# The entries of the feed-forward and MLP stages by token tile, and the gating units in single banks

## The reference

```python
x = x + rms_norm(h, norm_mix_post[i])
h = conv_gated_ffn(rms_norm(x, norm_ffn_pre[i]), ffn_w_in[i], ...)
# gating unit: 3072 features u and 3072 features v
z = jax.nn.gelu(h @ w_in)
u, v = jnp.split(z, 2, axis=-1)
v = layer_norm(v, ln_g, ln_b)            # over 3072 features
sv = einsum("gts,bcsgd->bctgd", tril(w_s), v) + b_s
return (u * sv) @ w_out
# MLP
f = jnp.square(jax.nn.relu(h @ w_up)) @ w_down
```

## Time and profile before

| | |
|---|---|
| median of 3 runs | 1098.77 us (1098.67 to 1100.65) |
| the profiled execution | 1098.5 us, its span 1096.7 us |
| instructions | 18812 |
| TensorE, VectorE, ScalarE busy | 97%, 74%, 61% |
| DMA | 185 MB, mean 169 GB/s |

### The profile page before, as it was taken

One profiled execution on the slowest core, in us unless ns is written; L12 is line 12 of the kernel. 1 busy time (PEld: TensorE's weight loads), 2 busy tenths in 40 slices (PEclk: granted clock), 3 DMA queues, 4 the chain that ended last, 5 costly groups with the idle time before them and its releaser, 6 DMA issues. The chain is left out here.

```text
span 1096.7 us, 18812 instructions
## 1 busy us (share of the span) xinstructions
PE 1069.3 (97%) x6166; PEld 912.2 (83%) x6166; DVE 814.1 (74%) x1427; ACT 669.0 (61%) x1246; POOL 39.8 (4%) x71
## 2 busy tenths in 40 slices
PE   7999999999999999999999999999999998999997
PEld 7977888888788998887888888899668887888886
DVE  6777988888744457886988888798779748666664
ACT  6666555555845855667555455777777756555543
POOL 0110000000010002220000000000000000000000
PEclk9999999999999999999999999999999999999999
DMA  8463665555466375442666656265212545655541
GB/s 330 136 218 121 206 215 186 184 192 183 133 246 192 126 231 163 154 153 78 228 201 200 191 175 195 84 221 173 77 39 79 186 141 171 190 184 187 189 153 38
DMA packets 51379, 185.03 MB, mean 169 GB/s; under 512 B 5728, under 2 KB 6240, under 8 KB 51328
## 3 DMA queue, kind: packets, MB, share of 16 engines
q1 hardware_dynamic: 49248, 178.28, 49.4%
q0 software_dynamic: 1504, 5.44, 1.5%
q10 hardware_dynamic: 576, 0.64, 0.2%
HBM read 183.29 MB, written 1.05 MB: 168 GB/s over the span
## 5 line engine op out<-in xcount | busy, mean ns | idle before, releaser
L156 DVE TENSOR_TENSOR w_lo<-raw,w_hi 128x1024 fp32r<-128x1024 f32 x336 | 415.3, 1245 | 85.3 <-ACT w_hi L151 82.0
L151 ACT ACTIVATE w_hi<-raw 128x1024 fp32r<-128x1024 f32 x336 | 350.0, 1053 | 81.1 <-PE ps L228 45.0
L198 PE MATMUL ps<-both,w_hi 128*128 128x512 f32 x960 | 341.9, 399 | 1.4 <-DVE both L436 1.4
L228 PE MATMUL ps<-w_hi,both 128*128 128x512 f32 x992 | 293.5, 396 | 6.0 <-DVE both L1264 2.4
L200 PE MATMUL ps<-both,w_lo 128*128 128x256 f32 x960 | 269.8, 281 | 0.0
L198 PEld LDWEIGHTS ps<-both,w_hi 128*128 128x128 f32 x960 | 180.5, 188 | 45.7 <-issue 2.0
L228 PEld LDWEIGHTS ps<-w_hi,both 128*128 128x128 f32 x992 | 178.8, 188 | 45.4 <-issue 3.4
L200 PEld LDWEIGHTS ps<-both,w_lo 128*128 128x128 f32 x960 | 181.6, 189 | 2.5
L228 PE MATMUL ps<-w_lo,both 128*128 128x512 f32 x496 | 158.3, 392 | 0.0
L173 PE MATMUL ps<-both,w_hi 128*128 128x256 f32 x448 | 128.8, 287 | 0.8 <-DVE arena L400 0.7
L174 PE MATMUL ps<-both,w_hi 128*128 128x256 f32 x448 | 126.9, 283 | 0.0
(11 more groups left out here) (202 smaller groups left out, 1119.0 us busy)
## 6 DMA issues: line engine op xcount, KB each, us to landing
raw<-in_w SPq DMA_DIRECT2D x336, 512.0 KB, 3.6
row<-in_rows POOLq DMA_DIRECT2D x7, 512.0 KB, 4.7
x<-in_x SPq DMA_DIRECT2D x2, 512.0 KB, 4.3
out<-x SPq DMA_DIRECT2D x4, 256.0 KB, 2.0
misc<-in_misc POOLq DMA_DIRECT2D x1, 512.0 KB, 6.1
arena<-in_ws POOLq DMA_DIRECT2D x1, 512.0 KB, 9.0
tab<-in_tables POOLq DMA_DIRECT2D x1, 320.0 KB, 4.7
tab<-in_tables POOLq DMA_DIRECT2D x1, 256.0 KB, 5.0
```

Source lines behind the costliest of these rows:

```text
L151: act.activation(w_hi[:, s, :], raw[:, s, :], ACT.Copy).then_inc(hi_done, 1)
L156: dve.tensor_tensor(w_lo[:, s, :], raw[:, s, :], w_hi[:, s, :].bitcast(F32), ALU.subtract).then_inc(lo_done, 1)
L198: pe.matmul(ps[:, bank, :].rearrange("p (h t) -> p h t", h=2), w_hi[:, s, c], both[:, :, k, :], start=k == 0, stop=False)
L228: mm = pe.matmul(ps[:, 2 * tt + c, :], a[:, slot, t], b[:, s, c * 512:(c + 1) * 512], start=f, stop=z)
```

## The change

- **Entries** (updates 0, 2, 4). `settle` and its dummy products go. `entry_pe` takes the sublayer's first two units apart by token tile with `features_tile`: tile 0 of unit n, half of the k of tile 0 of unit n + 1, then the transposes of tile 1, the other half, then tile 1 of both units. A k of a tile has a product of 256 columns (2 x 128) and one of 128, each with its own weight load. The feed-forward's row product comes one unit later, in bank 2; tile 0's gate and up banks are 0 and 1; tile 1 of x is transposed to banks 6, 7, 2, 3 at updates 0 and 2.
- **Weight halves.** At updates 0, 2 and 4 ScalarE makes the high halves of units n0 + 2 and n0 + 3 around the halves of x's tile 1 and VectorE their low halves behind them; units 4 and 5 come after the update. Update 4 takes the early order (both next squares behind those halves). The MLP's first three steps make two halves each in place of a block ahead of them.
- **Gating units.** u is made by `features_apart`, one unit to a bank (7, 0, 3 by turns). ScalarE copies the right half to `pad`, VectorE adds it to the left half into SBUF, multiplies a pair by ROW there, and ScalarE takes the gelu in place. A bank is free after the sum. The first output unit goes by token tile: tile 0 waits for the sum of unit 22, tile 1 for that of unit 23. The first three spatial products come two units later.
- **Squares by chunk.** A chunk's squares are taken one chunk later, about the chunk's own mean (`MID`); VectorE corrects them at the end to the common mean, by 512 times the square of the means' difference.

```diff
+    def features_tile(pe, n, bank, tt, pre, ks=range(KT)):
+
+        s = n % RING
+        pe.wait_ge(lo_done, n + 1)
+        o = ps[:, bank, :].rearrange("p (h t) -> p h t", h=2)
+        for k in ks:
+            pe.wait_ge(pre.lo, pre.base + k + 1)
+            c = slice(k * P, (k + 1) * P)
+            pe.matmul(o[:, :, tile(tt)], w_hi[:, s, c], both[:, :, k, tile(tt)], start=k == 0, stop=False)
+            mm = pe.matmul(o[:, 0, tile(tt)], w_lo[:, s, c], a_hi[:, k, tile(tt)], start=False, stop=k == KT - 1)
+        if tt == TT - 1:
+            mm.then_inc(unit_used, 1)
+
+    def entry_pe(pe, u, n, banks):
+
+        early, late = (Pre(u.next.lo, KT * (TT * u.n + tt)) for tt in range(TT))
+        features_tile(pe, n, banks[0], 0, early)
+        features_tile(pe, n + 1, banks[1], 0, early, range(KT // 2))
+        turn_tile_pe(pe, u, 1)
+        features_tile(pe, n + 1, banks[1], 0, early, range(KT // 2, KT))
+        features_tile(pe, n, banks[0], 1, late)
+        features_tile(pe, n + 1, banks[1], 1, late)
...
-    def spun(tt, k):
-
-        bank, c = (6, 7, 1, 2)[k // 2] if tt else 4 + k // 4, k % 2 if tt else k % 4
+    def spun(u, tt, k):
+
+        right = (6, 7, 2, 3) if u.n in (0, 2) else (6, 7, 1, 2)
+        bank, c = right[k // 2] if tt else 4 + k // 4, k % 2 if tt else k % 4
         return ps[:, bank, c * P:(c + 1) * P]
...
-    def update_act(act, u, g, following, early):
+    def update_act(act, u, g, following, early, ahead=RING):
...
+            if ahead == HELD:
+                hi_to(act, u.n_last + 3)
             hi_tile_act(act, u, 1, g)
+            if ahead == HELD:
+                hi_to(act, u.n_last + 4)
         next_act(act, u, 1)
         if following is not None:
             act.preload_act_table(following)
-        hi_to(act, u.n_last + RING)
-
-    def update_dve(dve, u, g, r, early, rows=None):
+        hi_to(act, u.n_last + ahead)
+
+    def update_dve(dve, u, g, r, early, rows=None, ahead=RING):
...
+        if early or ahead == HELD:
+            lo_to(dve, u.n_last + 4)
         if early:
-            lo_to(dve, u.n_last + 4)
             next_inverse(dve, u, 0)
         next_inverse(dve, u, 1)
         if rows is not None:
-            row_dve(dve, rows, 1)
-        lo_to(dve, u.n_last + RING)
+            lo_to(dve, u.n_last + 5)
+            row_dve(dve, rows, 2)
+        lo_to(dve, u.n_last + ahead)
...
-        return (0, 3) if t == 0 and isinstance(i, int) else (4 + t % 2, 6 + t % 2)
+        return (0, 1) if t == 0 and isinstance(i, int) else (4 + t % 2, 6 + t % 2)
     def ffn_pe(pe, f, n0, u, following, turn_early=True):
-        features_apart(pe, n0, 0, pre=after(u))
-        row_pe(pe, u, 1)
-        features_apart(pe, n0 + 1, 3)
-        ffn_in_pe(pe, f, n0, 1)
+        entry_pe(pe, u, n0, f_banks(0, 0))
+        features_apart(pe, f_g(n0, 1), f_banks(1, 0)[0])
+        row_pe(pe, u, 2)
+        features_apart(pe, f_g(n0, 1) + 1, f_banks(1, 0)[1])
...
-    UB = (7, 0, 1)
+    g_sem = signals("sgu", "v u u_part u_summed u_scaled masked rows rows_out stat square root centre vn mixed affine gated product hi lo")
+    UB = (7, 0, 3)
...
-        for p in range(3):
-            if p == 1:
-                pe.wait_ge(g_sem.v, 2 * SGC)
-            for k in range(2):
-                features(pe, N_SGU + 2 * p + k, ps[:, UB[p], k * SEQ:(k + 1) * SEQ])
-        def later_pair(p, i=0):
-            pe.wait_ge(g_sem.u, p - 2 + 3 * i)
-            for k in range(2):
-                features(pe, N_SGU + 2 * p + k, ps[:, UB[p % 3], k * SEQ:(k + 1) * SEQ], i)
-
+        def u_unit(m, i=0):
+            if m in (1, 2):
+                pe.wait_ge(g_sem.v, 8)
+            if m >= 3:
+                pe.wait_ge(g_sem.u_summed, m - 2 + 6 * i)
+            features_apart(pe, N_SGU + m, UB[m % 3], i)
+
+        for m in range(6):
+            u_unit(m)
         with pe.Fori(0, SGT // 6 - 2) as i:
-            for p in range(3, 6):
-                later_pair(p, i)
-        pe.wait_ge(next_sems.row_out, 2)
-        for j in range(3):
-            sgu_spatial(pe, j)
-        for p in range(SGT // 2 - 3, SGT // 2):
-            later_pair(p)
-        pe.wait_ge(g_sem.u, SGT // 2)
-
+            for m in range(6, 12):
+                u_unit(m, i)
+        for m in range(SGT - 6, SGT):
+            if m == SGT - 4:
+                for j in range(3):
+                    sgu_spatial(pe, j)
+            u_unit(m)
         def out_tile(j, i=0):
             pe.wait_ge(g_sem.lo, j + 1 + 6 * i)
             accumulate(pe, N_SGO + j, s_slot(j), j == 0, j == SGT - 1, i)
-        out_tile(0)
+        pe.wait_ge(g_sem.lo, 1)
+        for tt in range(TT):
+            pe.wait_ge(g_sem.u_summed, SGT - 1 + tt)
+            accumulate(pe, N_SGO, s_slot(0), True, False, tiles=(tt,))
...
+        def moments(c):
+
+            act.wait_ge(g_sem.centre, c + 1)
+            for tt in range(TT):
+                n = TT * c + tt
+                if n:
+                    act.wait_ge(g_sem.square, n)
+                k = 6 * tt + c
+                act.activation(G_PR[:, 0:2, :].rearrange("p a b -> p (a b)"), G_V[:, tt, c * 512:(c + 1) * 512],
+                               ACT.Square, bias=MID[:, k:k + 1],
+                               accum_out=lns[:, L_SQ + k:L_SQ + k + 1]).then_inc(g_sem.square, 1)
...
+            if c:
+                moments(c - 1)
...
         def pair(p, i, split):
-            split(0)
+            for k in range(2):
+                m = 2 * p + k
+                act.wait_ge(unit_used, N_SGU + m + 1 + 6 * i)
+                if m >= 2:
+                    act.wait_ge(g_sem.u_summed, m - 1 + 6 * i)
+                act.activation(pad[:, k, 2:2 + SEQ], ps[:, UB[m % 3], SEQ:2 * SEQ], ACT.Copy).then_inc(g_sem.u_part, 1)
+                split(k)
             act.wait_ge(g_sem.u_scaled, p + 1 + 3 * i)
-            dst = G_U[:, 2 * p:2 * p + 2, :] if isinstance(i, int) else G_U[:, bass.ds(2 * p + 6 * i, 2), :]
-            act.activation(dst.rearrange("p a b -> p (a b)"), ps[:, UB[p % 3], :],
-                           ACT.Gelu_apprx_tanh).then_inc(g_sem.u, 1)
-            split(1)
+            u = u_pair(p, i).rearrange("p a b -> p (a b)")
+            act.activation(u, u, ACT.Gelu_apprx_tanh).then_inc(g_sem.u, 1)
...
-        moments(0)
+        moments(SGC - 1)
         straight_pair(0)
-        moments(1)
+        act.wait_ge(g_sem.stat, 7)
+        act.activation(lns[:, L_ROOT:L_ROOT + 2], lns[:, L_VAR:L_VAR + 2], ACT.Sqrt).then_inc(g_sem.root, 1)
+        act.preload_act_table(ACT.Gelu_apprx_tanh)
         straight_pair(1)
-        act.wait_ge(g_sem.stat, 4)
-        act.activation(lns[:, L_ROOT:L_ROOT + 2], lns[:, L_VAR:L_VAR + 2], ACT.Sqrt).then_inc(g_sem.root, 1)
-        act.wait_ge(g_sem.stat, 6)
-        for j in range(3):
-            vn(j)
+        act.wait_ge(g_sem.stat, 9)
+        vn(0)
         straight_pair(2)
+        vn(1)
+        vn(2)
...
+        def pair_row(p, i=0, split=lambda j: None):
+            for k in range(2):
+                m = 2 * p + k
+                dve.wait_ge(g_sem.u_part, m + 1 + 6 * i)
+                dve.tensor_tensor(u_one(m, i), ps[:, UB[m % 3], 0:SEQ], pad[:, k, 2:2 + SEQ],
+                                  ALU.add).then_inc(g_sem.u_summed, 1)
+                if k == 0:
+                    split(0)
+            dve.wait_ge(g_sem.u_summed, 2 * p + 2 + 6 * i)
+            u = u_pair(p, i)
+            dve.tensor_tensor(u, u, ROW.rearrange("p (a t) -> p a t", a=1).to_broadcast([P, 2, SEQ]),
                               ALU.mult).then_inc(g_sem.u_scaled, 1)
-
-        lo_to(dve, N_SGV + 16)
-        row_dve(dve, 2, 6)
-        lo_to(dve, N_SGV + 4 * SGC - 1 + 6)
-        dve.wait_ge(g_sem.v, 2 * SGC)
+            split(1)
...
+        for c in range(SGC):
+            lo_to(dve, N_SGV + 4 * c + 8)
+            if c == 2:
+                row_dve(dve, 2, 6)
+            dve.wait_ge(g_sem.v, 2 * c + 2)
+            dve.tensor_scalar(mid[:, :, c:c + 1], two(L_SUM)[:, :, c:c + 1], -1.0 / 512, None,
+                              ALU.mult).then_inc(g_sem.centre, 1)
+            lo_to(dve, N_SGV + 4 * c + 9)
...
+        dve.wait_ge(g_sem.centre, SGC)
+        dve.tensor_tensor(two(L_SUM), mid, lns[:, L_NEG:L_NEG + 2].rearrange("p (a b) -> p a b", b=1)
+                          .to_broadcast([P, TT, SGC]), ALU.subtract).then_inc(g_sem.stat, 1)
         dve.wait_ge(g_sem.stat, 3)
+        dve.scalar_tensor_tensor(two(L_SUM), two(L_SUM), 512.0, two(L_SUM), ALU.mult,
+                                 ALU.mult).then_inc(g_sem.stat, 1)
...
+        dve.tensor_tensor(two(L_SQ), two(L_SQ), two(L_SUM), ALU.add).then_inc(g_sem.stat, 1)
+        dve.wait_ge(g_sem.stat, 5)
+        dve.tensor_reduce(lns[:, L_VSUM:L_VSUM + 2], two(L_SQ), AX.X, ALU.add).then_inc(g_sem.stat, 1)
...
+        pair_row(1, 0, lambda j: lo_to(dve, N_SGU + 8 + j))
+        pair_row(2, 0, lambda j: lo_to(dve, N_SGU + 10 + j))
...
-        def up(t, i=0, pre=None):
```

(38 more changed lines are left out.)

53 lines of the change are left out of this document (20 added, 33 removed).

## The result

The changed kernel takes 1090.79 us (1090.41 to 1091.02, 5 runs) beside 1100.43 for the kernel before in the same comparison (1098.67 to 1100.65, 5 runs): a ratio of 0.9921 [0.991, 0.9931]. Its profiled execution took 1090.79 with a span of 1089.0, so the two traces differ by 7.7 us in their spans (1096.7 before) and in their times. The medians differ by 9.6; where the other 1.9 comes from is the subject of the last experiment.

What follows compares the result with a forecast made beforehand. TensorE, busy 97% of the span at its upper clock, was taken as the bound. Gains 2.4 + 2.8 + 2.45 = 7.65 off 1098.5 gave 1090.85, plus 0.27 for the median: 1091.1 us, range 1087.5 to 1097.0.

Steps and rivals of the forecast that it cites:

- Tile passes: Narrow products at the entries: 0.23 us per step (0.116 + 0.113), 1.84 per pass of eight; bounds 0.17 and 0.66.
- A: Entry tile passes: the low-weight 128-column product runs at the plain rate, step 0.33, total 1096.8 us; chance 0.14.
- B: Entry tile passes: both products run at the plain rate, step 0.66, 29.7 us slower, 1128.5; chance 0.03.
- Entry of the feed-forward: Updates 0 and 2: TensorE gains 1.75 us, waiting for VectorE's up sum returns 0.5; 1.2 net each, 2.4 both.
- Entry of the MLP: Update 4: first down product near 917.85 instead of 920.63, so 2.8 us gained; bounds 2.1 and 3.85.
- Gating: Gating stage: shorter unit steps 1.2 us, less 0.2 for stalls, and 1.45 at its end; net 2.45.
- The squares: Moved into the value stage, covered by ScalarE's room; without it, 1.7 us a chunk delays a half wanted 14 later.
- C: VectorE's chains cut gains: 0.45 per feed-forward, 2.1 MLP, gating 0.5 and 1.4; 4.9 gained, 1093.9 us; chance 0.22.
- D: Entries and gating: TensorE alone decides, 10.85 us gained, 1087.9; chance 0.08.
- F: Whole kernel: something hides the change, leaving the time within 1 us of before; chance 0.05.
- E: Entries: the clock falls without the 24 dummy products; four passes at 1.2 GHz add 22.2 us, 1113.3; chance 0.03.

Runs made afterwards that it cites:

- the last experiment: The kernel before with only the changed entry of the last MLP (tile passes, spread weight halves, no dummy products there): 1096.04 us, ratio 0.9971.
- row_early: The changed kernel with the row product right behind the entry and its copy ahead of unit 4's low half: 1089.02 us, ratio 0.9908.
- all_three: row_early with two VectorE reorderings: gating unit 22's sum before two low halves, the MLP's first product low half before a weight's: 1088.66 us.
- squares_block: The changed kernel with all twelve squares behind the last chunk's gelus instead of one chunk later each: 1097.69 us, ratio 0.9981.
- full_width: The changed kernel with each entry's first two units at full width behind the transposes, weight halves still spread, no dummy products: 1098.75 us, ratio 0.999.
- no_dummies: The kernel before without its dummy products at updates 0, 2 and 4: 1100.32 us, ratio 1.0006.
- no_spread: The changed kernel with weight halves in their old places and the row product before unit 2, tile passes kept: 1098.76 us, ratio 0.9991.
- full_width_warm: full_width with the dummy products of the kernel before put back into the three gaps: 1095.04 us, ratio 0.9961.

## Why the prediction was right

**Total.** 1091.1 was forecast, 1090.79 measured. The sum was made against the profiled execution and gave 1090.85. That the sum, 7.65, met the 7.7 of the traces to 0.05 is luck in part: the three entries gave 5.81 where 5.2 was forecast, the gating 2.47 for 2.45, and the stretches forecast at nothing lost 0.58. I then added 0.27 for the median of three runs, two of the kernel's shorter kind and one of its longer. Had two been of the longer kind, the same step would have added 1.9 more. The 9.6 between the medians is 7.7 from the traces and some 1.9 from the clock; the forecast knew only the first. The forecast of the time stood, since the changed kernel's runs do not split.

**Tile passes.** 0.23 a step was right to the hundredth, but not by the split that I made. In the rows above the start after a 256-column product comes 0.17 later (97.02 to 97.19) and the one after a 128-column product 0.06 (to 97.25). What is even is the weight loads of the changed kernel:

```profile
97.07 0.19 PEld L212 LDWEIGHTS ps<-both,w_lo 128*128 128x128 f32 x1
97.20 0.19 PEld L211 LDWEIGHTS ps<-both,w_hi 128*128 128x128 f32 x1
97.31 0.19 PEld L212 LDWEIGHTS ps<-both,w_lo 128*128 128x128 f32 x1
```

A step is two of them, 0.115 each, so the nearest row, the transposes' pitch of 0.113, was the right one for both products. The Trainium skill (TensorE: Matmul & The Clock Gate, Back-to-back issue gap) gives 81 ns per product of 128 columns in a stream of loads and products; these traces do not agree, with 0.113 for the transposes and 0.115 here. The step of 0.23 refutes A and B.

**Entry of the feed-forward.** TensorE ends the passes at 101.2, forecast 100.9 and 0.28 for the late start. These are rows of VectorE in the changed kernel, which answer to the earlier trace rows:

```profile
105.40 1.22 DVE L156 TENSOR_TENSOR w_lo<-raw,w_hi 128x1024 fp32r<-128x1024 f32 x1
106.53 0.42 DVE L642 TENSOR_TENSOR arena<-ps,arena 128x256 f32<-128x256 f32 x1
...
115.71 0.41 DVE L656 TENSOR_TENSOR arena<-arena,ps 128x256 f32<-128x256 f32 x1
```

The first gate at 106.53 was forecast at 106.2 (and 0.28). The up sum starts at 115.71 and ends at 116.12, and its end was forecast at 115.8 (and 0.28). TensorE waits 0.47 for it (0.5 forecast). The net is 1.36 and 1.32 where 1.2 was said: the gate's product starts 0.06 behind the sum, and I had kept the 0.2 between its load and its product. row_early confirms the cause. A small slip stands in the working: 104.15, 0.42, 0.35 and 1.15 make 106.1, not 106.2.

**Entry of the MLP.** The chain was the forecast one, and its steps came up to 0.35 early. ScalarE's two square groups and VectorE's low halves were forecast to give down 0 at 917.85; 912.89 with the 4.61 by which this kernel was ahead at the last held product is 917.50. So 3.13 for 2.8. What was left of the wait, 0.52, was forecast near 1. The larger part of the gain came from the spread and not from the passes, 2.0 against 1.1: with the halves in their old place the wait is 2.84.

**Gating.** The total, 2.47 for 2.45, is right by two errors that cancel. The units gave 1.48, not 1.0: there were none of the stalls I had taken off, and a step is 0.353 in the middle of the stage but 0.347 in its last unit, the lower end of what I had allowed. The end gave 0.99, not 1.45: I had counted on the first tile's banks being free with the last unit but one, but its sum (L1260, unit 22) waited on VectorE behind two weight low halves. These are VectorE's rows there:

```profile
418.01 2.83 DVE L156 TENSOR_TENSOR w_lo<-raw,w_hi 128x1024 fp32r<-128x1024 f32 x2
420.76 0.41 DVE L1330 TENSOR_TENSOR both<-arena,both 128x256 fp32r<-128x256 f32 x1
421.10 0.95 DVE L1260 TENSOR_TENSOR arena<-ps,pad 128x256 f32<-128x256 f32 x2
```

TensorE's first output product starts at 421.61. The view puts its wait down to L1330, which ends at 421.17; the first of the two sums ends some 0.4 later and is the operand that TensorE needed. In all_three, with that sum ahead of the low halves, the wait is gone.

The squares were costed at nothing with the value stage as their cover, and at 1.7 a chunk, beside 14 us to spare, without it. squares_block shows what the order of before would cost with single banks: 6.9.

**Rivals.** C is refuted: the entries gave 1.36, 1.32 and 3.13 where it had 0.45, 0.45 and 2.1, and its stalls in the gating did not come (no wait there between 350 and 420). Only at the gating's end was VectorE later than even C had it, 0.99 for 1.4. D was refuted by the waits of 0.47, 0.35 and 0.52, F by the 7.7. E had the right mechanism at the wrong place: the clock does fall in such a gap, as full_width and no_dummies show, but the change fills the gap with products, and with its eight transposes of 1.08 us between two passes the clock stays at 1.00. Its price was far too high: three such gaps cost 3.7 in full_width where E had 22.2. The rule of the Trainium skill (TensorE: Matmul & The Clock Gate, Part 4: PE-mode transpose) that transposes do not count as busy in the same way was therefore not put to the test by this kernel.

## What to carry to other kernels

If TensorE idles while a norm is made ready, look for work that needs only the half which is ready: narrower products take a third more of TensorE's time (7.4 for 5.6 here) but take it where the engine was idle. Then walk the helper engine's queue behind it, because it becomes the bound in the same microsecond; here neither the passes nor the new order of the weight halves gained anything alone at the feed-forwards, and together they gained 1.3 each. And look at the rows behind a wait of some us, which show whether the clock fell: where it did, the wait cost more than its length.

## What the runs showed that was not expected

- The clock behind a wait. TensorE's granted clock stood below 1.00 behind the idle gaps of 3.04 to 3.08 (six of six), 2.84 and 5.07 us, and stayed at 1.00 behind those of 1.77, 1.78 and 1.03, and behind the one of 4.6 to 5.1 with which every traced run starts. At the one of 2.02 it was 1.00 in the profiled run, and by the times of 53 runs it fell in about three of five (33). The price was 3.7 for three gaps in full_width and 2.8 behind down 0 in no_spread. In the kernel before, whose wait at down 0 absorbs a part, it was 1.0 by the profiled executions and 2.0 by the medians of no_dummies and of the shorter runs of before.
- Dummy products in the gap hold the clock at 1.00 but do no work; real products in their place gave 4.25 us more (full_width_warm against the changed kernel).
- In a tile pass the weight loads follow each other evenly, one every 0.115 us, though the products between them have 256 and 128 columns by turns. So it seems to be the loads and not the columns that set the step of 0.23; no run took that apart.
